# The last round of a mixture-of-experts kernel: halves, grouped roots, and a wait of VectorE on GpSimd

## The reference, cut to what matters

```python
h = silu(xb @ w_gate[e]) * (xb @ w_up[e])      # xb: the tokens of one block, e its expert
acc = acc.at[tok].add((h @ w_down[e]) * g[:, None])
...
x = layer_norm(ALPHA * x + moe, ln2_g, ln2_b)  # ((x - mu) * rsqrt(var + eps)) * g + b
```

## Time and profile before

| | us |
|---|---|
| median of 3 runs | 1223.3 (1221.96 to 1224.83) |
| profiled execution, its own time | 1224.56 |
| its span in the trace | 1222.8 |
| TensorE busy | 1172.9 (96%) |
| VectorE busy | 525.7 (43%) |
| ScalarE busy | 342.7 (28%) |
| GpSimd busy | 167.4 (14%) |

### The profile page before, as it was taken

The page is one execution under the profiler, slowest core; times in us unless marked ns, Lnnn a source line. Parts: engine busy times, 40 slices in busy tenths (PEclk is TensorE's granted clock), DMA queues, the critical chain, the costliest instruction groups (busy, mean ns, idle before and its releaser), DMA issues.

```text
span 1222.8 us, 26865 instructions
## 1 busy us (share of the span) xinstructions
PE 1172.9 (96%) x11263; PEld 558.1 (46%) x11263; DVE 525.7 (43%) x983; ACT 342.7 (28%) x546; POOL 167.4 (14%) x222
## 2 busy tenths in 40 slices
PE   7999999999989999999899999899999999999995
PEld 3444444444557776777544444333333333333331
DVE  7166532144538777777335456711111111111147
ACT  1044312333335556555532112000010000000044
POOL 4122400000012221121000001011011011011021
PEclk9999999999999999999999999899999999999998
DMA  5111101110000100100270862699779948998566
GB/s 224 52 50 35 37 34 52 35 35 18 0 2 4 38 3 3 38 4 3 71 293 1 329 241 103 238 364 386 286 232 330 332 124 295 348 321 292 172 189 225
DMA packets 63067, 178.40 MB, mean 146 GB/s; under 512 B 3296, under 2 KB 3424, under 8 KB 62960
## 3 DMA queue, kind: packets, MB, share of 16 engines
q1 hardware_dynamic: 56560, 153.70, 34.3%
q0 software_dynamic: 6400, 23.11, 7.3%
HBM read 152.68 MB, written 24.12 MB: 145 GB/s over the span
## 4 chain that ended last, share of the span: by engine, by line
PE 85%; DVE 6%; ACT 3%; issue 3%; DMA 3%; POOL 0%; POOLq 0%; DVEq 0%; SPq 0%; ACTq 0%
PE PS L2202 29%; PE PS L249 10%; PE PS L361 8%; PE PS L1480 8%; PE PS L370 3%; PE PS L822 3%; PE PS L347 3%; PE PS L1157 2%; PE PS L841 2%; PE PS L1166 2%; PE PS L1176 2%; DMA YT<-x1d,RK 2%; PE PS L2182 2%; PE PS L506 1%; PE PS L897 1%
## 5 line engine op out<-in xcount | busy, mean ns | idle before, releaser
L2202 PE MATMUL PS<-ALL,YT 128*32 128x512 f32 (+1 forms) x3648 | 401.7, 596 | 6.3 <-issue 4.6
L2202 PEld LDWEIGHTS PS<-ALL,YT 128*32 128x32 f32 x3648 | 127.8, 110 | 264.5 <-issue 263.6
L1480 PE MATMUL PS<-SQ,YT 128*128 128x512 f32 x256 | 114.3, 596 | 0.6 <-issue 0.6
L2390 DVE TENSOR_TENSOR YT<-YT,PS 128x256 f32<-128x256 f32 x38 | 14.3, 417 | 226.1 <-PE PS L2202 226.1
L361 PE MATMUL PS<-XS 128*128 128x512 f32 x224 | 97.4, 593 | 0.0
L1480 PEld LDWEIGHTS PS<-SQ,YT 128*128 128x128 f32 x256 | 47.7, 190 | 58.9 <-issue 57.8
L361 PEld LDWEIGHTS PS<-XS 128*128 128x128 f32 x224 | 42.3, 190 | 54.4 <-issue 53.9
L2156 POOL DMA_INDIRECT sums<-YT,RK x18 | 29.1, 1617 | 237.0 <-DVE YT L2410 237.0
L2410 DVE TENSOR_SCALAR YT<-PS,RK 128x512 f32<-128x512 f32 x18 | 13.5, 750 | 106.1 <-PE PS L2202 106.1
L822 PE MATMUL PS<-XS 64*64 64x64 f32 x1920 | 48.0, 227 | 7.9 <-ACT XS L979 6.8
L822 PEld LDWEIGHTS PS<-XS 64*64 64x64 f32 x1920 | 37.1, 134 | 25.2 <-ACT XS L979 12.5
(11 more groups left out here) (474 smaller groups left out, 1629.1 us busy)
## 6 DMA issues: line engine op xcount, KB each, us to landing
ALL<-in_w_gate SPq DMA_DIRECT2D x16, 2048.0 KB, 13.7
ALL<-in_w_upx SPq DMA_DIRECT2D x16, 2048.0 KB, 12.4
ALL<-in_w_down SPq DMA_DIRECT2D x16, 2048.0 KB, 20.1
XS<-in_w_in SPq DMA_DIRECT2D x21, 512.0 KB, 3.6
XS<-in_xT SPq DMA_DIRECT2D x16, 512.0 KB, 10.8
x1d<-RK SPq DMA_DIRECT2D x9, 512.0 KB, 10.1
SQ<-in_w_out SPq DMA_DIRECT2D x8, 512.0 KB, 4.4
RK<-in_x SPq DMA_DIRECT2D x8, 512.0 KB, 6.6
```

What stands on the lines that cost most here:

```text
L1480: ins = e.matmul(PS[i % 2][:, half * HB:(half + 1) * HB], YT[:, kt, i * P:(i + 1) * P], WO[kt][:, half * HB:(half + 1) * HB], start=kt == ...
L2202: ins = e.matmul(acc[r, :], rows[:, r], right, start=start, stop=stop)
```

## The change

Five things are done.

1. The down product signals `s_y1` after each half, not after both. ScalarE's `gated` (left half) waits for the left half alone; VectorE's still for both. The other waits on `s_y1` are doubled so that they mean the same rounds as before. This holds in all rounds.
2. Behind the last round, the product of the left half of `LAST_Y` with the token matrix waits for ScalarE's half only, that of the right half for VectorE's.
3. ScalarE's roots are taken for several tiles by one pair of instructions, and moved: moments 3, `gated`, moments 4 and 5, load of the Ln and Exp table, roots 0 to 2, roots 3 to 5, silu of the last round, moments 6 and 7, the table again, roots 6 and 7, the copy of line 2341, moments and root 8, `gated`, root 9.
4. VectorE's list is put in another order: gains 0 and 1 ahead of the `gated` of round `rounds`, then gains 2 to 5, biases 0 to 2, a wait on the semaphore `s_iota` until GpSimd has issued both gathers of line 2171, biases 3 and 4, hidden product, copy, gate, bias 5, then gain and bias of tiles 6, 7 and 8, and only then the `gated` of the last block.
5. For tile 9 each half is added and then at once given to the statistics, in the place of both additions and then both statistics.

The diff, cut:

```diff
@@ moe_pool
             for k in range(2):
                 e.indirect_dma_start(FIN[NT + k], None, sums, ...last_rows[:, k:k + 1]...).then_inc(s_ug, 16)
+            e.sem_inc(s_iota)
@@ down_products
-            if half == 1 and f == FT - 1:
+            if f == FT - 1:
                 ins.then_inc(s_y1, 1)
@@ moe_pe
             e.wait_ge(s_same, 5)
-            e.wait_ge(s_ya, rounds + 3)
-            e.wait_ge(s_yd, rounds + 3)
             for half in range(2):
+                e.wait_ge((s_ya, s_yd)[half], rounds + 3)
                 e.matmul(last_sums[:, half * HB:(half + 1) * HB], same, LAST_Y[:, half * HB:(half + 1) * HB],
@@ moe_act
             e.wait_ge(s_ys, rounds * 16 + 16)
-            for i in range(BY_DVE, BY_DVE + 2):
+            final_moments_act(e, BY_DVE)
+            gated(rounds, Yb)
+            for i in range(BY_DVE + 1, NT - 2):
                 final_moments_act(e, i)
-            gated(rounds, Yb)
-            for i in range(BY_DVE + 2, BY_DVE + 4):
+            exp_ln(e)
+            final_roots(e, 0, BY_DVE)
+            final_roots(e, BY_DVE, NT - 2)
+            hidden(rounds + 1)
+            for i in range(NT - 2, NT):
                 final_moments_act(e, i)
-            hidden(rounds + 1)
             exp_ln(e)
-            for i in range(BY_DVE + 4):
-                final_root(e, i)
+            final_roots(e, NT - 2, NT)
             hidden_turned(rounds + 1)
-            for i in range(BY_DVE + 4, NT + 1):
-                final_moments_act(e, i)
-                final_root(e, i)
+            final_moments_act(e, NT)
+            final_roots(e, NT, NT + 1)
             gated(rounds + 1, LAST_Y)
-            final_root(e, NT + 1)
+            final_roots(e, NT + 1, NT + 2)
@@ moe_dve
             final_gain(e, 0)
+            final_gain(e, 1)
             gated(rounds, Yb)
...
-            for i in range(1, BY_DVE + 4):
+            for i in range(2, NT - 2):
                 final_gain(e, i)
             for i in range(3):
+                final_bias(e, i)
+            e.wait_ge(s_iota, 2)
+            for i in range(3, 5):
                 final_bias(e, i)
             hidden(rounds + 1)
             hidden_turned(rounds + 1)
             gate_of(rounds + 1)
-            for i in range(3, NT - 1):
+            final_bias(e, 5)
+            for i in range(NT - 2, NT + 1):
+                final_gain(e, i)
                 final_bias(e, i)
-            final_gain(e, NT - 1)
-            final_bias(e, NT - 1)
             gated(rounds + 1, LAST_Y)
-            final_gain(e, NT)
-            final_bias(e, NT)
             last_rows_dve(e)
-            final_moments_dve(e, NT + 1)
             final_gain(e, NT + 1)
             final_bias(e, NT + 1)
@@ last_rows_dve
                 e.tensor_tensor(x[:, cols], x[:, cols], last_sums[:, cols], ALU.add).then_inc(s_same, 1)
+                wait(e, s_same, 6 + half)
+                e.bn_stats(st[:, 6 * half:6 * half + 6], x[:, cols]).then_inc(s_f1, 1)
+            wait(e, s_f1, MOMENTS[NT + 1] - 1)
+            e.bn_aggr(m[:, 0:2], st).then_inc(s_f1, 1)
+        def final_roots(e, a, b):
+            spread_of, roots = mv[:, a:b, 1:2], mv[:, a:b, 2:3]
+            moments_done(e, b - 1)
+            e.activation(roots, spread_of, ACT.Ln, ...).then_inc(s_n2a, 1)
+            wait(e, s_n2a, ROOTS[a] - 1)
+            e.activation(roots, roots, ACT.Exp, scale=-0.5).then_inc(s_n2a, 1)
```

More of the change, by code:

```diff
@@ L643, in rw_pe @@
                 heads_sum(e, PS[3], Y).then_inc(s_rp, 1)
-        s_iota = sem("iotas_by_pool")
+        s_iota = sem("iotas_or_last_gathers_begun_pool")
         ip = TT[:, 0, 0:P].bitcast(I32)
@@ L2096, in moe_sp @@
             wait(e, s_tab, 1)
-            e.wait_ge(s_y1, table(e, T_END + 1, MAXR, 1) + 1)
+            e.wait_ge(s_y1, table(e, T_END + 1, MAXR, 1) * 2 + 1)
             e.sem_inc(s_tick[0])
@@ L2104, in released @@
                 if n % 3 == 2:
-                    e.wait_ge(s_y1, r + 1)
+                    e.wait_ge(s_y1, r * 2 + 1)
                 else:
@@ L2339, in hidden_turned @@
                 e.wait_ge(s_htp2, i + 2)
-                e.wait_ge(s_y1, i + 1)
+                e.wait_ge(s_y1, i * 2 + 1)
                 e.copy(HhT[:, 2 * P:4 * P], PS[2][:, HB:HB + 2 * P]).then_inc(s_hta, 1)
@@ L2347, in gated @@
             def gated(i, y):
-                e.wait_ge(s_y1, i + 2)
+                e.wait_ge(s_y1, i * 2 + 2)
                 e.wait_ge(s_gc, i + 1)
@@ L2408, in gated @@
                 e.wait_ge(s_gc, i + 1)
-                e.wait_ge(s_y1, i + 2)
+                e.wait_ge(s_y1, i * 2 + 3)
                 e.tensor_scalar_mul(y[:, HB:2 * HB], PS[3][:, HB:2 * HB], cur_gate).then_inc(s_yd, 1)
@@ L2471, in layer_kernel @@
         spare = TT[:, 2, :]
[L2473 to L2480, removed]
+        MOMENTS = {0: 2, 1: 4, 2: 6, NT + 1: 9}
+        ROOTS = {0: 2, 1: 2, 2: 2, 3: 4, 4: 4, 5: 4, 6: 6, 7: 6, NT: 8, NT + 1: 10}
         def last_rows_dve(e):
-            x = FIN[NT + 1]
+            x, st, m = FIN[NT + 1], stats[:, (NT + 1) % 2, :], mv[:, NT + 1, :]
             wait(e, s_ug, 32)
@@ L2489, in last_rows_dve @@
                 e.tensor_tensor(x[:, cols], x[:, cols], last_sums[:, cols], ALU.add).then_inc(s_same, 1)
-        def dve_moments(i):
-            return i if i < BY_DVE else BY_DVE if i == NT + 1 else None
+                wait(e, s_same, 6 + half)
+                e.bn_stats(st[:, 6 * half:6 * half + 6], x[:, cols]).then_inc(s_f1, 1)
+            wait(e, s_f1, MOMENTS[NT + 1] - 1)
+            e.bn_aggr(m[:, 0:2], st).then_inc(s_f1, 1)
         def final_moments_dve(e, i):
             x, st, m = FIN[i], stats[:, i % 2, :], mv[:, i, :]
-            moments_ready(e, i)
-            k = dve_moments(i)
+            wait(e, s_x[i], 32)
             for half in range(2):
@@ L2502, in final_moments_dve @@
             ins.then_inc(s_f1, 1)
-            wait(e, s_f1, 2 * k + 1)
+            wait(e, s_f1, MOMENTS[i] - 1)
             e.bn_aggr(m[:, 0:2], st).then_inc(s_f1, 1)
@@ L2508, in final_moments_act @@
             x, m, n = FIN[i], mv[:, i, :], i - BY_DVE
-            moments_ready(e, i)
+            if i < NT:
+                wait(e, s_x[i], 32)
+            else:
+                wait(e, s_ug, 32)
             wait(e, s_f2, 3 * n)
@@ L2515, in final_moments_act, with moments_done @@
             e.activation(spare, x, ACT.Square, scale=-1.0, bias=m[:, 0:1], accum_out=m[:, 1:2]).then_inc(s_f2, 1)
[L2517 to L2521, removed]
+        def moments_done(e, i):
+            if i in MOMENTS:
+                wait(e, s_f1, MOMENTS[i])
             else:
                 wait(e, s_f2, 3 * (i - BY_DVE + 1))
-            e.activation(m[:, 2:3], m[:, 1:2], ACT.Ln, scale=1.0 if dve_moments(i) is not None else 1.0 / D, bias=consts[:, 3:4])\
+        def final_roots(e, a, b):
+            spread_of, roots = mv[:, a:b, 1:2], mv[:, a:b, 2:3]
+            moments_done(e, b - 1)
+            e.activation(roots, spread_of, ACT.Ln, scale=1.0 if a in MOMENTS else 1.0 / D, bias=consts[:, 3:4])\
              .then_inc(s_n2a, 1)
-            wait(e, s_n2a, 2 * i + 1)
-            e.activation(m[:, 2:3], m[:, 2:3], ACT.Exp, scale=-0.5).then_inc(s_n2a, 1)
+            wait(e, s_n2a, ROOTS[a] - 1)
+            e.activation(roots, roots, ACT.Exp, scale=-0.5).then_inc(s_n2a, 1)
         def final_gain(e, i):
@@ L2532, in final_gain @@
             wait(e, s_l2, 32)
[L2533 to L2536, removed]
+            moments_done(e, i)
             e.scalar_tensor_tensor(x, x, m[:, 0:1], LN2[0], ALU.subtract, ALU.mult).then_inc(s_f3, 1)
@@ L2541, in final_bias @@
             x, m = FIN[i], mv[:, i, :]
-            wait(e, s_n2a, 2 * (i + 1))
+            wait(e, s_n2a, ROOTS[i])
             wait(e, s_f3, i + 1)
```

## The result

Over 19 runs of each kernel the changed one took 1225.66 us (median; 1223.16 to 1229.08), the one before 1223.63 (1221.6 to 1226.01). The ratio is 1.0017 with an interval of 1.0009 to 1.0024: about 2.0 us slower, where 0.9 faster was forecast.

A forecast was written before the change was run, and what follows sets the result against it. VectorE's list behind the last hidden product was taken to set the end. Tail +1.41 - 2.58 + 0.17 = -1.00, GpSimd's wait +0.1, sum -0.9 us; from the median of 1223.3 that gave 1222.4 us, range 1220.6 to 1224.5.

The forecast's parts named there:

- Rounds in the loops: 0: Looped rounds: ScalarE's half is done 3.5 us sooner, but the scatter waits for VectorE's half; SyncE's doubled counts also 0.
- The tail's sum, -1.00: VectorE behind the last hidden product: seven passes +1.41, gain 8 and bias 8 gone -2.58, tile 9 by halves +0.17.
- the 4.3 that I took: Second gather's landing behind the last hidden product: taken as by 1203.5, so that gain 8 would not wait.
- The rival of the late gather: Tile 8: ScalarE or the second gather is late, VectorE idles before gain 8; price 0.5 us, time 1222.9, chance 0.17.
- the rival on GpSimd's wait: Last hidden product late by the scatter's landing and gathers: 1224.2 at 8.9 us landing, 1225.8 at 10.5; chance 0.13.
- The wait on GpSimd: VectorE ahead of biases 3 and 4 and the last hidden product: held until about 1196.6; +0.1 us, +0.45 if longer.
- the slower rival: GpSimd's wait takes the place of the gain: late scatter landing delays the last hidden product; 1224.2 us, chance 0.13.
- just in time: Tile 9: the right token product takes 0.98 us, done at 1211.45, before the right addition could start at 1211.63.
- The interference on GpSimd's issues: GpSimd beside VectorE: by the Trainium skill's exclusion rule the first gather waits for bias 2's rest, time 0.3 us longer.
- ScalarE's two extra table loads: ScalarE ahead of the line 2341 copy: silu's load and a second Ln and Exp load, 0, at worst +0.5 us.
- the drain of 1.38: ScalarE's table switches: by the skill about 2.66 us each, bias 6 0.4 late, time 1222.8; chance 0.03.
- the 0.2% that had 0.86 of the chance: Whole kernel: about 2.4 us can be told from no change; same 0.86, faster 0.08, slower 0.06.

The follow-up runs named there:

- own_sem: The changed kernel with a semaphore of its own for the left half, s_y1 counting whole products, no doubled counts; 1223.18 us, ratio to before 0.9998.
- before_doubled: The kernel before, with the down product signalling after each half and all waits on s_y1 doubled, nothing else; ratio to before 1.0014.
- after_swapped: The changed kernel with the two waits ahead of the copies of turned hidden rows exchanged, on VectorE and ScalarE; ratio to before 1.0007.
- own_sem_hold3: As own_sem, but SyncE keeps the stores of tiles 3 to 7 back until both last gathers have landed; ratio to before 0.9993.
- own_sem_true_wait: As own_sem, but VectorE's awaited signal comes from a small GpSimd memset behind both gathers, not from its sequencer; ratio to before 0.9992.
- own_sem_hold: As own_sem, but SyncE keeps all eight stores back until both last gathers have landed; ratio to before 1.0014.
- after_again: The changed kernel unaltered, run again for a second profile; ratio to before 1.0020.
- own_sem_no_wait: As own_sem, with VectorE's wait for GpSimd ahead of biases 3 and 4 taken out; ratio to before 1.0000.

## Why the prediction was wrong

- **The step that failed** is "Rounds in the loops: 0". I priced the early signal and SyncE's doubled counts, and never asked what `i * 2 + 1` costs on VectorE, where two waits stand ahead of an instruction that TensorE waits for. The register instruction that it brings there costs 0.10 us in each round, 1.7 us in all; own_sem, before_doubled and after_swapped show it from three sides.
- **The tail's sum, -1.00, was right** as VectorE's list: 16.99 against 18.06 in own_sem_hold3 is -1.07. The changed kernel didn't get it, since the second gather lands at 6.0 and not at the 4.3 that I took. I had written that stores leaving earlier would lie less beside it; more was moved beside it. From 1196 to 1205 the DMAs moved 384 GB/s in the changed kernel and 328 before; with all stores held back it was 283, and the gather landed first. The rival of the late gather was there, at 0.5; it costs 1.05, the whole gain.
- In the rival on GpSimd's wait, 1.9 at a landing of 8.9 us holds only if the second gather takes 1.63; with 0.94 it is 1196.6 + 1.5 + 2.4 - 1199.25 = 1.25, and with 1.63 the gain is used up by a landing 0.55 later, not 0.9. own_sem_true_wait, at 8.6 and with gathers of 0.94, bears out the smaller figure.
- **The wait on GpSimd** I took as a wait for finished gathers. It is met when GpSimd's sequencer has passed both, before the second is made. As written it costs nothing (forecast 0.1). Where it does what its words say, the slower rival appears in one execution of two, 0.91 us.
- **The right token product** "just in time" came out with its length mis-sized: one token product by itself takes 1.13, not the 0.98 taken from half of a pair. It was still in time in every profile of this order but the first of the changed kernel, where TensorE's clock had fallen: 0.58 of waiting, and 0.7 in the tail. Why it fell there is open.
- **The interference on GpSimd's issues.** I held it against the rule that the prediction cites that the issues were lengthened by less than one pass. But an issue that starts inside a pass has only the rest of it to wait for, and that fits: the scatter of the earlier trace rows began 0.55 ahead of the end of a VectorE pass and was lengthened by 0.42, the second gather began 0.82 ahead and was lengthened by 0.69, 0.13 less than the rest each time. The first gather of the changed kernel began 0.26 ahead of the end of bias 2 and took 1.07, 0.13 longer than alone. It held nothing up, since VectorE's wait did not reach so far.
- **ScalarE's two extra table loads** were hidden, as forecast: the copy of line 2341 stayed within its cover. Each load took 1.28 us and the next instruction started 0.02 behind (below); the drain of 1.38 that the Trainium skill (ScalarE: Activation LUTs, What ACT_TABLE_LOAD costs) adds does not show.
- The parts add up, nearly: 1.7 for the rounds, and 0.0 and 0.7 for the tail in the two profiles, against 2.0 measured. How often the tail is the longer one is not settled.
- The measured 0.17% lies within the 0.2% that had 0.86 of the chance, but the range ended 1.2 us too low: it was built from the tail alone.

ScalarE's table load in the changed kernel, for the point on the drain:

```profile
1187.77 1.28 ACT L402 ACT_TABLE_LOAD   x1
1189.07 0.30 ACT L2526 ACTIVATE RK<-RK,consts 128x3 f32<-128x3 f32 x1
```

## What to carry to other kernels

Ahead of an instruction that another engine waits for, keep the wait that blocks as the last one and on the instruction itself; a wait against a computed count, placed behind it, costs 0.1 us in every round. A second event deserves a second semaphore, rather than a doubled count in every loop. Before transfers are moved earlier, ask which later transfer shares the DMAs with them and what is due from it; and a signal from a sequencer behind a software-made DMA doesn't say that the DMA has been made.

## What the runs showed of the hardware

- A register instruction that carries the blocking wait ahead of VectorE's copy costs 0.10 us (0.20 to 0.30 idle; before against before_doubled, own_sem and after_swapped against the changed kernel).
- A semaphore increment of GpSimd's sequencer behind two indirect DMAs released VectorE 0.29 us behind the start of the first and 0.95 ahead of the second (own_sem_hold). A memset with the increment on it, behind the same DMAs, ended at 1196.79, and VectorE started at 1196.82 (own_sem_true_wait).
- TensorE's half clock followed idle times of 1.07 and 1.13 us in one profile (1.81 us for two passes). After 1.05 and 1.13 in after_again, and 1.49 and 1.13 in after_swapped, the clock stayed and they took 1.13 and 1.12. What decides is not shown.
- An indirect gather takes 0.94 us if it starts beside an idle VectorE. Of the 28 gathers of line 2171 in the 14 profiles, 20 start during a VectorE pass with two SBUF inputs. 15 of these end 0.81 or 0.82 us behind the end of the pass in which they start (durations of 0.95 to 1.67), and 3 that start in its last 0.1 us end 0.86 or 0.87 behind it. Where a next pass follows, it starts beside the gather and still takes its 1.28, so VectorE is not seen to be held up. The other two, in own_sem and own_sem_no_wait, end 0.81 behind the third pass and take 3.69 and 3.64. The Trainium skill (SBUF — State Buffer, Who interferes with whom) has a VectorE instruction with two SBUF inputs and a reading GpSimd instruction exclude each other. GpSimd's side of that agrees here; VectorE's does not show. In which gap between passes GpSimd gets in, the runs don't settle.
- The same gather of 512 KB landed in 5.6 us with no stores about (own_sem_hold), in 6.9 with the stores of tiles 0 to 2 (own_sem_hold3) and in 9.7 with every store sent as soon as its tile is ready (the changed kernel).
